# A mixed stage in a one-layer decoder step: the first query batch, the page table, the peer keys and two page groups move into the stage before it

## The chip, the cores and the metric

The kernel runs on one NeuronCore of a Trainium2 chip, in one launch. Its time is the device time of the whole execution in microseconds (us); lower is better. The engines are TensorE (PE; its weight loads are PEld), VectorE (DVE), ScalarE (ACT), GpSimd (POOL) and SyncE (SP); here SyncE only issues DMAs and waits for them, and its queue is SPq in the rows. Each engine works off its own instruction stream in order, and semaphores tie the streams together.

## The reference

One inference step of a one-layer decoder for a prompt of 1024 tokens and 8 samples of 8 new tokens, model width 1024. Only what the change touches stands here:

```
mix = concat([attention, rglru], -1) @ w_out
x1 = layer_norm(alpha * x + mix, ln1_g, ln1_b)
ffn = peer_ffn(x1, peer_wq, peer_keys, peer_u, peer_v)
...
def block(tb):                                   # 128 tokens
    q = (tb @ wq).reshape(128, 8, 2, 128)        # 8 retrieval heads, two halves
    sc = jnp.einsum('thpd,hpnd->thpn', q, keys)  # 128 keys for each half
    s1, i1 = lax.top_k(sc[:, :, 0], 16)
    s2, i2 = lax.top_k(sc[:, :, 1], 16)
    cand = s1[..., :, None] + s2[..., None, :]
    top_s, top_p = lax.top_k(cand, 16)           # 16 of 16384 experts
    g = softmax(top_s)
    act = gelu(einsum('td,thkd->thk', tb, u_tab[eidx]))
    return einsum('thk,thkd->td', g * act, v_tab[eidx])
...
past_k = cache_k[page_table]                     # samples: 32 pages of 128 keys each
```

The attention is differential (two softmax maps per head). Everything is float32.

## The kernel before

The kernel is a row of blocks. A block ends when all five engines have arrived at a barrier, and the next begins there.

**The mix block** (function `prompt_attention_mix`, up to 654 us) computes the prompt's attention, and then, for eight tiles of 128 tokens in the order `TILES` = 4 to 7, 0 to 3, the product with `w_out` on TensorE (`half_mix`, L877) and the layer norm on VectorE (last instruction L1077). This is x1. It lies in `res[g % 2]` and SyncE stores it to `x1_scratch` in DRAM (L783), waits until the store has landed, and loads the x row for the tile after next. The first four of these tiles, the *dense* ones, are also transposed into `x1Td` in SBUF. Three slices of the query weights `peer_wq` (one per retrieval head) are loaded into the ring `ring` here. The PSUM banks `S[0]` and `S[1]` (`a_s`) take the products of alternate tiles.

**The mixed stage** (first block of `peer`, 654 to 1461 us) is laid out in slots by a planner that runs when the program is built. All engines walk the slots in the same order. Each of the eight samples has 32 slots:

- *Sample attention.* In slots 0 to 15 of a sample TensorE transposes its 32 key pages (`page_turn_pe`, L1557), ScalarE copies them out (L1567), and every fourth page is followed by scores. Slot 16: scores of the new keys (L1589). Slots 17 to 19: softmax on VectorE (it makes `cj`, L1608, the scale of the weights) and the exponential on ScalarE. Slots 20 to 31: the weights' transposes (L1621) and the products with the value pages. The pages come in groups of four (`GP`) through a ring `pg` in `w_room`; SyncE reads each page's number from `pt`, the page table in SBUF, before it issues the load. `pt` is loaded at the block's start.
- *Queries.* 16 batches of 16 matmuls of 128x512 each (`q_pe`, L1320), placed by the table `Q_AT`: 8 in each of slots 0 and 1, none in slots 2 to 7, after that mostly one in a slot, three in slots 16 to 19 of a sample. A batch is one head for four tiles. Batches of *dense* tiles read `x1Td`; batches of *gathering* tiles (0 to 3) read `x1T[1]`, which is made in slots 9 and 10 (`X_TURN_AT`) by transposes (L1285) of x1 rows that SyncE loads back from `x1_scratch` (`load_xn`); VectorE (L1294) and ScalarE copy them out. ScalarE copies each half batch of queries (L1328), TensorE multiplies with the transposed keys (`score_pe`, L1369), ScalarE copies the scores (L1377).
- *Keys.* The 16 key matrices are loaded by two DMAs at the second page group and transposed in slots 2 and 3 (`KEY_TURN_AT`); ScalarE copies them (L1307).
- *Ranking*, on VectorE, 17 steps for each batch (`RANK_STEPS`): eight searches of 16 best (`top16`, L1382 to L1389), the pairs (L1402, L1405), four more searches, place, index twice, gate (L1482). Its slots come out of a planner with a cost for each step. The first batch is ranked in slots 5 to 15.
- *Scatters*, on GpSimd: when a dense batch is ranked, 48 indirect DMAs of 128 gates each (`scatter_pool`, L1782) add them into `gate_scratch` in DRAM, for three of the four dense tiles; eight heads make 384. The fourth dense tile's gates become one-hot matrices on VectorE and ScalarE in the last sample's slots and after (`QUAD_AT`), and matmuls on TensorE (L1839).
- *End.* After slot 255 the samples' outputs are folded by TensorE in slot 257 (L1857, behind VectorE's L2000), mixed, normalised, and one more small batch of queries and scores is made. SyncE then loads the first gates (L2031, L2036).

**The last stage** (1461 us to the end) runs 128 chunks of 128 experts for the dense tiles on TensorE (L2044 transposes, L2058 and L2090 products) and beside it the gathers of 16 experts per token and head for the other tiles on GpSimd, with VectorE.

A q step (one matmul of 128x512) has two records in the trace, a transpose has one.

## Time and profile before

| what | value |
|---|---|
| median of 3 runs | 3581.18 us |
| the runs | 3580.72, 3581.18, 3588.79 us |
| profiled execution, its own time | 3575.43 us |
| its span in the trace | 3573.7 us |
| TensorE busy over the span | 3357.5 us (94%) |
| VectorE busy | 2622.8 us (73%) |
| GpSimd busy | 2051.8 us (57%) |
| ScalarE busy | 842.2 us (24%) |
| DMA, mean over the span | 286 GB/s |
| mixed stage | 654.2 to 1461.3 us |
| last stage | 1461.3 to 3573.7 us |

The trace is of one execution, with times from the span's start. Busy shares are means over stages with different limits. A timeline row stands for one or more like instructions of an engine: when they start, how long they last in all, and in brackets the idle time of the engine just before them and what ended it. Granted clock means the share of TensorE's full clock that the chip gave in that stretch.

### The profile page before, as it was taken

To read this page: it belongs to the slowest core of one execution; us is meant where nothing else is said; L and a number is where in the kernel's file an instruction comes from. 1 tells how busy PE (TensorE), PEld (TensorE's weight loads), DVE (VectorE), ACT (ScalarE), POOL (GpSimd) and SP (SyncE) were. 2 spreads that over 40 slices of the span, in tenths; PEclk is the share of its full clock that TensorE was granted. 3 is DMA by queue.
4 is the path that set the end of the run, shared out by engine and by line. 5 is a ranking of instruction groups with operands and counts; after the bars stand their busy time and mean duration, and the time that the engine had idled before them with its cause. 6 is when DMAs were issued, how large, how long until landed. Compare 5 with 4: busy or idle time off the path is not lost.

```text
span 3573.7 us, 41306 instructions
## 1 busy us (share of the span) xinstructions
PE 3357.5 (94%) x12551; PEld 1744.3 (49%) x12551; DVE 2622.8 (73%) x5429; ACT 842.2 (24%) x1786; POOL 2051.8 (57%) x1620
## 2 busy tenths in 40 slices
PE   8999799799899977799999999999999999999898
PEld 5676464444444445444444444444444444444343
DVE  3444584467778766578887888888888888888884
ACT  2333560344443465111111111111111111111021
POOL 0000100078888888577777777777777677777540
PEclk9999899899999988899999999999999999999999
DMA  4000631588889885899999999999999999999961
GB/s 148 30 29 15 243 146 68 179 213 213 205 211 233 226 229 147 263 396 407 405 407 398 400 406 404 403 394 406 406 406 404 396 391 407 405 401 398 355 218 42
DMA packets 410615, 1023.34 MB, mean 286 GB/s; under 512 B 93965, under 2 KB 130030, under 8 KB 406834
## 3 DMA queue, kind: packets, MB, share of 16 engines
q0 software_dynamic: 221184, 604.27, 46.6%
q1 hardware_dynamic: 175138, 394.69, 31.5%
q10 hardware_dynamic: 14096, 22.02, 1.7%
q8 instruction: 90, 1.47, 0.2%
q14 instruction: 107, 0.88, 0.1%
HBM read 972.05 MB, written 48.77 MB: 286 GB/s over the span
## 4 chain that ended last, share of the span: by engine, by line
POOL 21%; DMA 19%; issue 9%; DVE 7%; PE 2%; ACT 0%; DVEq 0%; SPq 0%; ACTq 0%; POOLq 0%
DMA u<-in_peer_u,idx_all 19%; POOL v L2165 11%; POOL u L2157 10%; DVE u L2175 2%; DVE facc L2203 2%; PE e_b L2319 1%; PE e_b L2090 1%; DVE wq L2203 1%; DMA w_room<-x_scratch 1%; DVE k_room L2105 1%; PE e_b L2307 0%; DVE ln_st L1060 0%; DVE w_room L2389 0%; DVE w_room L1073 0%; DVE w_room L2360 0%
## 5 line engine op out<-in xcount | busy, mean ns | idle before, releaser
L2157 POOL DMA_INDIRECT u<-in_peer_u,idx_all x576 | 724.8, 1258 | 393.2 <-DVE act L2175 246.4
L2090 PE MATMUL e_b<-w_room,e_room 128*128 128x512 f32 x2048 | 908.1, 597 | 21.7 <-DVE k_room L2105 12.8
L2175 DVE CUSTOM_DVE_ANT_0 u<-u,xb 128x1024 f32<-128x1024 f32 x576 | 705.7, 1225 | 295.1 <-DMA u<-in_peer_u,idx_all 268.5
L2058 PE MATMUL e_b<-wq 128*128 128x512 f32 x2048 | 900.3, 592 | 0.0
L2165 POOL DMA_INDIRECT v<-in_peer_v,idx_all x576 | 690.5, 1199 | 214.1 <-issue 177.5
L1782 POOL DMA_INDIRECT gate_scratch<-e_room,slot_of x384 | 610.4, 1590 | 188.3 <-issue 120.9
L2090 PEld LDWEIGHTS e_b<-w_room,e_room 128*128 128x128 f32 x2048 | 390.9, 191 | 519.4 <-issue 491.8
L2058 PEld LDWEIGHTS e_b<-wq 128*128 128x128 f32 x2048 | 379.5, 190 | 429.0 <-issue 429.0
L2203 DVE SCALAR_TENSOR_TENSOR facc<-v,w,facc 128x1024 f32<-128x1024 f32 x317 | 406.5, 1282 | 1.4
L2203 DVE SCALAR_TENSOR_TENSOR wq<-v,w,wq 128x1024 f32<-128x1024 f32 x254 | 325.9, 1283 | 0.5
L2051 ACT ACTIVATE wq<-e_b 128x512 f32<-128x512 f32 x256 | 140.0, 594 | 722.3 <-PE e_b L2044 473.2
L2064 ACT ACTIVATE wq<-e_b 128x512 f32<-128x512 f32 x128 | 76.5, 597 | 745.3 <-PE e_b L2058 599.7
L812 POOL MEMSET qz<- 128x1024 f32 x1 | 1.0, 951 | 375.8 <-POOLq L110 375.8
L445 PE MATMUL p_bank<-w_in,wq 128*128 128x512 f32 (+1 forms) x432 | 186.9, 592 | 0.0
L2105 DVE TENSOR_TENSOR k_room<-k_room,e_b 128x512 f32<-128x512 f32 x248 | 158.4, 678 | 6.7 <-PE e_b L2090 6.7
L2044 PEld LDWEIGHTS e_b<-ident,wq 128*128 128x128 f32 x1024 | 121.0, 142 | 80.0 <-issue 79.9
L1567 ACT ACTIVATE w_room<-e_b 128x512 f32<-128x512 f32 x256 | 139.8, 597 | 55.0 <-PE e_b L1557 46.8
L2044 PE MATMUL e_b<-ident,wq 128*128 128x128 f32 x1024 | 134.4, 275 | 12.9 <-PEq L2398 12.9
L2319 PE MATMUL e_b<-wq,e_room 128*128 128x512 f32 (+1 forms) x288 | 133.7, 620 | 13.4 <-DVE w_room L2379 6.9
L1320 PE MATMUL e_b<-wq 128*128 128x512 f32 x256 | 128.2, 615 | 11.4 <-PEq L110 11.1
L1320 PE MATMUL e_b<-v,wq 128*128 128x512 f32 x256 | 132.5, 621 | 0.9 <-PE e_b L1648 0.7
L439 PE MATMUL p_bank<-wq,w_in 128*128 128x128 f32 (+1 forms) x1152 | 132.0, 277 | 0.9 <-issue 0.9
(387 smaller groups left out, 3543.4 us busy)
## 6 DMA issues: line engine op xcount, KB each, us to landing
wq<-in_peer_u SPq DMA_DIRECT2D x128, 512.0 KB
w_room<-in_peer_v SPq DMA_DIRECT2D x128, 512.0 KB, 22.6
w_room<-in_cache_v SPq DMA_DIRECT2D x144, 256.0 KB
w_room<-in_cache_k SPq DMA_DIRECT2D x128, 256.0 KB
gate_scratch<-zeros SPq DMA_DIRECT2D x24, 1024.0 KB, 27.0
wq<-gate_scratch SPq DMA_DIRECT2D x96, 256.0 KB
u<-in_cache_k SPq DMA_DIRECT2D x64, 256.0 KB
xb<-in_cache_k SPq DMA_DIRECT2D x64, 256.0 KB
```

The costliest lines, as they stand in the source:

```text
L445: last = pe.matmul(bank[0:R, :], xT[:, k, 0:R], w_in[:, k, col:col + AW], start=(k == 0), stop=(k == KC - 1))
L1320: last = pe.matmul(B[m][:], ring[h % NR][:, k, m * P:m * P + P], x1T[group][:, k, :], start=(k == 0), stop=(k == KC - 1))
L1782: pool.indirect_dma_start(gate_d[m].rearrange("e (t o) -> (e t) o", o=1), bass.IndirectOffsetOnAxis(ap=slot_of[:, m, h, j:j + 1], axis=0), ...
L2044: last = pe.transpose(TQ[r][:, k * P:k * P + P], Ud[c % NUD][:, at:at + P], ident[:])
L2058: last = pe.matmul(AQ[c % 2][:, 0:DT], UT[c % 2][:, k, :], x1Td[:, k, :], start=(k == 0), stop=(k == KC - 1))
L2090: last = pe.matmul(OQ[i % 2][b][:], WT[n % 2][:, c, m * P:m * P + P], Vd[(4 * n + c) % NVD][:, b * 512:b * 512 + 512], start=(c == 0), sto ...
L2105: dve.tensor_tensor(part, part, OQ[i % 2][b][:], ALU.add).then_inc(s["dadd"], 1)
L2157: pool.indirect_dma_start(u[x % NU], None, a["peer_u"], bass.IndirectOffsetOnAxis(ap=idx_all[:, t, h, j:j + 1], axis=0)).then_inc(s_u[x % ...
L2165: pool.indirect_dma_start(v[y % NV], None, a["peer_v"], bass.IndirectOffsetOnAxis(ap=idx_all[:, t, h, j:j + 1], axis=0)).then_inc(s_v[y % ...
L2175: dve.tensor_tensor_reduce(u[x % NU], u[x % NU], xb[t % 2][:], 1.0, 0.0, ALU.mult, ALU.add, act16[k % 2][:, j:j + 1]).then_inc(s["ufree"], 1)
L2203: dve.scalar_tensor_tensor(out=dst, in0=v[y % NV], scalar=w, in1=dst, op0=ALU.mult, op1=ALU.add).then_inc(s["vfree"], 1)
L2319: last = pe.matmul(Z[h][0:R, :], x2T[q % 2][:, k, 0:R], wg[:, k, h * 512:h * 512 + 512], start=(k == 0), stop=(k == KC - 1))
```

## The change

1. **First queries.** The 16 matmuls of batch 0 are issued at the end of TensorE's part of the mix block, after the last `half_mix`. They write to the banks of `S[0]`, which now live on as `q_banks` into the next block. In that block `Q_AT` begins with batch 1: two matmuls in each of slots 2 to 9, none in 10 to 15, then the old pattern. ScalarE copies batch 0's queries in slots 0 and 1, its scores are made in slots 1 and 2, and its ranking goes to slots 1 to 11 (was 5 to 15). By the planner's rules all other batches come earlier too: batch 13, the last dense one, is ranked by slot 214 (was 223), the last batch in slots 233 to 247 (was 244 to 267).
2. **Early loads.** SyncE loads the page table at the mix's start, the keys after the first x1 store (into `keys_in`), and the first two page groups, eight pages, after the second and the third (into `early`), all in free room of `wq`. The ring of page groups is counted from the third on.
3. **Stores of x1.** The last two are no longer waited for on SyncE in the mix; their landing is waited for by GpSimd at the start of the next block and by SyncE before it loads x1 rows.
4. **Keys and x1 transposes.** `KEY_TURN_AT` has all four key steps in slot 0, `X_TURN_AT` all four tiles in slot 15, and the loads of x1 rows for it come with page group 6 instead of groups 1 and 2.

```diff
             def load_early(sp, g):
+                if g == 0:
+                    kv = a["peer_keys"].rearrange("(g q p) d -> g p q d", q=8, p=P)
+                    for n in range(2):
+                        sp.dma_start(keys_in[:, n, :].rearrange("p (q d) -> p q d", q=8), kv[n]).then_inc(s_early, 16)
+                elif g <= NEARLY:
+                    if g == 1:
+                        sp.wait_ge(s_pt, 16)
+                    for n in range(GP):
+                        at = (g - 1) * GP + n
+                        page = sp.value_load(pt[0:1, at:at + 1], min_val=0, max_val=a["cache_k"].shape[0] // PAGE - 1)
+                        sp.dma_start(early[g - 1][:, n, :], a["cache_k"][bass.ds(page * PAGE, PAGE), :]
+                                     ).then_inc(s_early, 16)
...
                 for g in range(NT):
                     sp.wait_ge(sx["x1"], g + 1)
-                    sp.dma_start(rows(x1_d, TILES[g] * P, P), res[g % 2][:]).then_inc(s_st[g % 2], 16)
-                    sp.wait_ge(s_st[g % 2], 16 * (g // 2 + 1))
+                    done = s_st[g % 2] if g + 2 < NT else s_x1st
+                    sp.dma_start(rows(x1_d, TILES[g] * P, P), res[g % 2][:]).then_inc(done, 16)
+                    load_early(sp, g)
                     if g + 2 < NT:
+                        sp.wait_ge(done, 16 * (g // 2 + 1))
                         sp.wait_ge(sx["xt"], 2 * min(g + 1, NDT))
                         load(g + 2)
...
+                pe.wait_ge(sx["sum"], NT - 1)
+                pe.wait_ge(sx["xe"], 2 * NDT)
+                pe.wait_ge(s_wq[0], 16)
+                for m in range(2):
+                    for k in range(KC):
+                        pe.matmul(B[0][m], ring[0][:, k, m * P:m * P + P], x1Td[:, k, :],
+                                  start=(k == 0), stop=(k == KC - 1))
...
-        KEY_TURN_AT = {2: (0, 1), 3: (2, 3)}
-        X_TURN_AT = {9: (0, 1), 10: (2, 3)}
+        KEY_TURN_AT = {0: (0, 1, 2, 3)}
+        X_TURN_AT = {15: (0, 1, 2, 3)}
...
-            n = 8 if x < 2 else 0 if x < 8 else 3 if 16 <= c < 20 else 0 if c % 8 == 7 or c in (3, 11, 27) else 1
+            n = 0 if x < 2 else 2 if x < 10 else 0 if x < 16 else 3 if 16 <= c < 20 else 0 if c % 8 == 7 or c in (3, 11, 27) else 1
...
-            ready = Q_DONE[e, 1] + 4
+            ready = Q_DONE[e, 1] + 4 if e else 1
...
                 def rows_between(G):
-                    if G == 1:
-                        kv = a["peer_keys"].rearrange("(g q p) d -> g p q d", q=8, p=P)
-                        for g in range(2):
-                            sp.dma_start(v[6 + g].rearrange("p (q d) -> p q d", q=8), kv[g]).then_inc(s["kr"], 16)
-                        for n in range(2):
+                    if G == NEARLY + NPB:
+                        sp.wait_ge(s_x1st, 32)
+                        for n in range(UN):
                             load_xn(sp, n)
-                    if G == 2:
-                        for n in range(2, UN):
-                            load_xn(sp, n)
-
-                sp.dma_start(pt[:], a["page_table"]).then_inc(s["pt"], 16)
-                sp.wait_ge(s["pt"], 16)
+
+                sp.wait_ge(s_pt, 16)
...
             @block.gpsimd
             def _(pool):
+                pool.wait_ge(s_x1st, 32)
                 pool.memset(qst, 0.0)
```

TensorE, from the last product of the mix into the mixed stage, before (L1320 are queries, L1557 page transposes):

```order
L877 MATMUL a_s<-w_out,mixA 128x512 [waits s_p_r]
L877 MATMUL a_s<-w_out,mixA 128x512 x7
L779 UNCONDITIONAL_BRANCH
L2448 UNCONDITIONAL_BRANCH [waits barrier_Pool_Activation_PE_DVE_SP_release]
L1320 MATMUL e_b<-wq 128x512 [waits s_wq0]
L1320 MATMUL e_b<-wq 128x512 x7
L1557 MATMUL e_b<-ident,w_room 128x128 [waits s_p_hc]
L1557 MATMUL e_b<-ident,w_room 128x128 x3
L1557 MATMUL e_b<-ident,w_room 128x128 [waits s_p_hc]
L1557 MATMUL e_b<-ident,w_room 128x128 x3
L1320 MATMUL e_b<-wq 128x512 x8
```

and now (L947 are queries, L1336 key transposes, L1597 page transposes):

```order
L904 MATMUL a_s<-w_out,mixA 128x512 [waits s_p_r]
L904 MATMUL a_s<-w_out,mixA 128x512 x7
L947 MATMUL q_banks<-wq 128x512 [waits s_wq0,s_dve,s_pool]
L947 MATMUL q_banks<-wq 128x512 x15
L803 UNCONDITIONAL_BRANCH
L2484 UNCONDITIONAL_BRANCH [waits barrier_Pool_Activation_PE_DVE_SP_release]
L1336 MATMUL e_b<-ident,wq 128x128 [waits s_early]
L1336 MATMUL e_b<-ident,wq 128x128 x7
L1336 MATMUL e_b<-ident,wq 128x128 [waits s_e_kte]
L1336 MATMUL e_b<-ident,wq 128x128 x3
L1336 MATMUL e_b<-ident,wq 128x128 [waits s_e_kte]
L1336 MATMUL e_b<-ident,wq 128x128 x3
```

The sixteen query matmuls stand ahead of the block's end, and the new block opens with sixteen key transposes ahead of the first pages.

ScalarE, from the start of the mixed stage, before (L1548 and L1550 the sample's queries and keys, L1567 page copies, L1328 query copies, L1307 key copies):

```order
L2453 UNCONDITIONAL_BRANCH [waits barrier_Pool_Activation_PE_DVE_SP_release]
L1548 ACTIVATE w_room<-qTs 64x8 [waits s_e_zero,s_e_S]
L1548 ACTIVATE w_room<-qTs 64x8 x7
L1550 ACTIVATE w_room<-kTs 128x32
L1567 ACTIVATE w_room<-e_b 128x4x128 [waits s_e_ktp,s_e_S]
L1567 ACTIVATE w_room<-e_b 128x4x128 [waits s_e_ktp]
L1328 ACTIVATE k_room<-e_b 128x512 [waits s_e_q]
L1567 ACTIVATE w_room<-e_b 128x4x128 [waits s_e_ktp] x2
L1307 ACTIVATE k_room<-e_b 128x512 [waits s_e_kt] x2
L1328 ACTIVATE k_room<-e_b 128x512 [waits s_e_q]
```

and now (L1341 key copies, L1362 query copies, L1588 and L1590 the sample's queries and keys, L1607 page copies, L1411 score copies):

```order
L1341 ACTIVATE k_room<-e_b 128x512 [waits s_e_kt,s_e_zero]
L1341 ACTIVATE k_room<-e_b 128x512 [waits s_e_kt] x3
L1362 ACTIVATE k_room<-q_banks 128x512
L1588 ACTIVATE w_room<-qTs 64x8 [waits s_e_S]
L1588 ACTIVATE w_room<-qTs 64x8 x7
L1590 ACTIVATE w_room<-kTs 128x32
L1607 ACTIVATE w_room<-e_b 128x4x128 [waits s_e_ktp,s_e_S]
L1607 ACTIVATE w_room<-e_b 128x4x128 [waits s_e_ktp]
L1362 ACTIVATE k_room<-q_banks 128x512
L1607 ACTIVATE w_room<-e_b 128x4x128 [waits s_e_ktp] x2
L1411 ACTIVATE e_room<-e_b 128x512 [waits s_e_sc]
```

Keys and queries are copied first, the sample's queries behind them, and the first score copy comes right after the fourth page copy.

VectorE, in the middle of the first batch's ranking, before (L1382 to L1389 a search, L1294 copies of transposed x1, L1402 and L1405 the pairs):

```order
L1387 MAX tv<-wq 128x8 [waits s_e_ch]
L1389 MAX_INDEX ti<-tv,wq 128x8 [waits s_e_ch]
L1294 COPY v<-e_b 128x4x128 [waits s_e_xt] x2
L1402 CAST tif<-ti 128x128 [waits s_e_ch]
L1405 TENSOR_TENSOR wq<-tv 128x4x64
L1405 TENSOR_TENSOR wq<-tv 128x4x48
L1294 COPY v<-e_b 128x4x128 [waits s_e_xt,s_e_ch]
L1294 COPY v<-e_b 128x4x128 [waits s_e_xt]
L1382 MAX ts<-wq 128x8
```

and now (L1416 to L1423 a search, L1436 and L1439 the pairs):

```order
L1421 MAX tv<-wq 128x8 [waits s_e_ch]
L1423 MAX_INDEX ti<-tv,wq 128x8 [waits s_e_ch]
L1436 CAST tif<-ti 128x128 [waits s_e_ch]
L1439 TENSOR_TENSOR wq<-tv 128x4x64
L1439 TENSOR_TENSOR wq<-tv 128x4x48
L1416 MAX ts<-wq 128x8 [waits s_e_ch]
```

The copies of transposed x1 no longer stand between the searches.

## Rows read from the trace of the kernel before

**Rows 1.** Stretches of 100 us: length, busy PE, PEld, DVE, ACT, POOL, granted clock, DMA share, GB/s.

```profile
700.00:800.00 100.00, 93.31 (x549) 48.20 (x547) 70.13 (x282) 46.47 (x91) 66.79 (x43) 1.00 0.81 209
1700.00:1800.00 100.00, 100.00 (x276) 47.35 (x275) 83.82 (x117) 11.44 (x23) 72.85 (x59) 1.00 1.03 406
```

**Rows 2.** GpSimd's timeline (start, duration), first and last scatter; their group on the page.

```profile
720.19 1.74 POOL L1782 DMA_INDIRECT gate_scratch<-e_room,slot_of  x1 [65.42 <-DVE e_room L1482]
...
1451.91 1.54 POOL L1782 DMA_INDIRECT gate_scratch<-e_room,slot_of  x1 [0.30 <-issue]
...
L1782 POOL DMA_INDIRECT gate_scratch<-e_room,slot_of x384 | 610.4, 1590 | 188.3 <-issue 120.9
```

**Rows 3.** Timelines of TensorE and SyncE at the mixed stage's end; SyncE's waits.

```profile
1447.30 1.09 PE L1369 MATMUL e_b<-k_room 128*64 128x128 f32 x16 [0.79 <-ACT k_room L1377]
...
1461.30 3.81 PE L2044 MATMUL e_b<-ident,wq 128*128 128x128 f32 x16 [12.91 <-PEq L2398]
...
1449.43 0.45 SPq L2031 DMA_DIRECT2D wq<-gate_hot  x1
...
1455.49 3.74 SPq L2036 DMA_DIRECT2D wq<-gate_scratch  x3
...
SPq L2036 <- DMA gate_scratch<-e_room,slot_of: 8.3, 3, 5.6
```

**Rows 4.** TensorE's timeline from the mix's last product into the mixed stage.

```profile
636.14 7.03 PE L877 MATMUL a_s<-w_out,mixA 128*128 128x512 f32 x16
...
654.25 9.78 PE L1320 MATMUL e_b<-wq 128*128 128x512 f32 x16 [11.08 <-PEq L110]
...
664.74 7.03 PE L1320 MATMUL e_b<-wq 128*128 128x512 f32 x16
```

**Rows 5.** VectorE and SyncE there; SyncE's wait for stores (sum, count, longest).

```profile
648.89 1.22 DVE L1077 TENSOR_TENSOR res<-res,b 128x1024 f32<-128x1024 f32 x1
...
SPq L783 <- DMA x_scratch<-res: 4.4, 2, 2.2
...
665.90 3.66 SPq L1532 DMA_DIRECT2D w_room<-in_cache_k  x4
```

**Rows 6.** VectorE's timeline, the ranking of batch 0.

```profile
682.30 0.30 DVE L1382 MAX8 tv<-e_room 128x8 f32<-128x128 f32 x1 [26.90 <-ACT e_room L1377]
...
694.88 0.67 DVE L1294 COPY v<-e_b 128x512 f32<-128x512 f32 x1
...
697.49 0.69 DVE L1405 TENSOR_TENSOR wq<-tv 128x256 f32<-128x256 f32 x2
...
703.46 0.27 DVE L1382 MAX8 ts<-wq 128x8 f32<-128x112 f32 x1
...
719.67 0.23 DVE L1482 TENSOR_TENSOR e_room<-e_room,zx 128x64 f32<-128x64 f32 x1
```

**Rows 7.** ScalarE's first row of the stage; the page copies' group on the page.

```profile
654.92 1.74 ACT L1548 ACTIVATE w_room<-qTs 64x8 f32<-64x8 f32 x8 [8.37 <-POOL pcol L2443]
...
L1567 ACT ACTIVATE w_room<-e_b 128x512 f32<-128x512 f32 x256 | 139.8, 597 | 55.0 <-PE e_b L1557 46.8
```

**Rows 8.** A stretch of 10 us at the stage's start, columns as in rows 1.

```profile
650.00:660.00 10.00, 5.75 (x7) 2.45 (x8) 0.68 (x5) 1.88 (x9) 0.53 (x3) 0.52 0.28 98
```

**Rows 9.** TensorE's timeline at single places; its wait for the weights' scale.

```profile
695.60 1.11 PE L1285 MATMUL e_b<-ident,v 128*128 128x128 f32 x4 [3.63 <-DVE v L1294]
...
706.10 1.12 PE L1557 MATMUL e_b<-ident,w_room 128*128 128x128 f32 x8 [0.40 <-ACT w_room L1567]
...
721.34 0.25 PE L1589 MATMUL e_b<-w_room 128*32 128x8 f32 x8 [0.72 <-issue]
...
1295.27 0.25 PE L1589 MATMUL e_b<-w_room 128*32 128x8 f32 x8 [0.83 <-ACT wq L1584]
...
1356.47 3.33 PE L1857 MATMUL e_b<-w_room,sel 128*32 128x512 f32 x4 [7.95 <-DVEq L2000]
...
PE e_b L1621 <- DVE cj L1608: 10.2, 4, 4.0
```

More of the change, by code:

```diff
@@ L50 @@
 NR = 3
+GP = 4
+NEARLY = 2
 NSC = 3
@@ L138, in program @@
         room = wq[:].rearrange("p k n -> p (k n)")
+        early = [room[:, (10 + 2 * n) * D:(12 + 2 * n) * D].rearrange("p (g d) -> p g d", g=GP) for n in range(NEARLY)]
+        keys_in = room[:, 14 * D:16 * D].rearrange("p (n d) -> p n d", n=2)
         kT, qT, v_all, spare = [room[:, n * 4 * D:(n + 1) * 4 * D] for n in range(4)]
@@ L742, in prompt_attention_mix @@
         res = [sb(f"res{n}", [P, D]) for n in range(2)]
-        S = [ps(f"a_s{m}", (P, 2 * 512)) for m in range(2)]
+        S = [q_banks, ps("a_s1", (P, 2 * 512))]
         TB = [ps(f"a_t{n}") for n in range(2)]
@@ L1232, in peer @@
         ln2 = LayerNorm(sb, sem, "ln2", g2, b2)
-        B = [ps(f"e_b{n}") for n in range(8)]
+        B = [q_banks[:, 512 * n:512 * n + 512] for n in range(2)] + [ps(f"e_b{n}") for n in range(2, 8)]
         ACC, QB, TB, KB, SB_, OB = B[0:2], B[2], B[3], B[4:6], B[6], B[7]
@@ L1301, in keys_pe @@
                 m = 4 * t + c
-                last = pe.transpose(B[2 + t % 2][:, c * P:c * P + P], v[6 + m // 8][:, (m % 8) * P:(m % 8) * P + P], ident[:])
+                last = pe.transpose(B[2 + t % 2][:, c * P:c * P + P], keys_in[:, m // 8, (m % 8) * P:(m % 8) * P + P], ident[:])
             last.then_inc(s["kt"], 1)
@@ L1325, in q_act @@
         def q_act(act, e, m):
-            act.wait_ge(s["q"], 2 * e + m + 1)
+            wait(act, s["q"], 2 * (e - 1) + m + 1)
             wait(act, s["sc"], 2 * (e - 2) + 2)
@@ L1355, in score_pe @@
                 pe.wait_ge(s["kte"], 4)
-            if e == 1 and r == 0:
+            if e == 2 and r == 0:
                 pe.wait_ge(s["xTa"], UN)
@@ L1519, in pages @@
                 at = turn_of(i, G)
-                dst, done = (late_pages, s_late) if G == LATE_G else (pg[at % NPB], s_pg[at % NPB])
+                if at < NEARLY:
+                    continue
+                room = (at - NEARLY) % NPB
+                dst, done = (late_pages, s_late) if G == LATE_G else (pg[room], s_pg[room])
                 src = a["cache_k"] if G < NG else a["cache_v"]
@@ L1527, in pages @@
                 for n in range(GP):
-                    if G != LATE_G and at >= NPB:
+                    if G != LATE_G and at >= NPB + NEARLY:
                         page_free(sp, at - NPB, n)
@@ L1538, in page_group @@
             at = turn_of(i, G)
+            if at < NEARLY:
+                return early[at]
+            at -= NEARLY
             pe.wait_ge(s_pg[at % NPB], 16 * GP * (at // NPB + 1))
@@ L1696, in peer @@
         Q_AT, Q_DONE = {}, {}
-        x, step = Q_FIRST, 0
+        Q_DONE[0, 0] = Q_DONE[0, 1] = 0
+        x, step = Q_FIRST, 2 * KC
         while step < NBAT * 2 * KC:
             c = x % SEQ_SLOTS
-            n = 8 if x < 2 else 0 if x < 8 else 3 if 16 <= c < 20 else 0 if c % 8 == 7 or c in (3, 11, 27) else 1
+            n = 0 if x < 2 else 2 if x < 10 else 0 if x < 16 else 3 if 16 <= c < 20 else 0 if c % 8 == 7 or c in (3, 11, 27) else 1
             for _ in range(min(n, NBAT * 2 * KC - step)):
@@ L1720, in peer @@
         for e in range(NBAT):
-            ready = Q_DONE[e, 1] + 4
+            ready = Q_DONE[e, 1] + 4 if e else 1
             for name, n in RANK_STEPS:
-                first_slot = ready + (2 if name == "top" and n >= 4 else 0)
+                first_slot = ready + ((2 if e else 1) if name == "top" and n >= 4 else 0)
                 if slot < first_slot:
```

30 lines of the change are left out of this document (19 added, 11 removed), and 2 rows, old and new, of the table names.

## The prediction

> **What bounds the kernel now.** I read the stretches of the whole span first. In the last of the kernel's stages TensorE is busy 100.00 of 100 us [rows 1]; there the order of work is the same before and after, so what starts it earlier should end it earlier. In the stage ahead of it, in which the sample attention, the queries and the ranking are mixed (I call it the mixed stage; it runs from 654.2 to 1461.3 us), no engine is full: TensorE 93, VectorE 70, GpSimd 67 of 100 us [rows 1]. So I went to the two ends of that stage, and asked which chain ends last.
>
> The timeline of GpSimd [rows 2] shows one unbroken chain. It sits idle 65.42 us until the first batch's last ranking step, scatters for the first time at 720.19, and for the last time at 1451.91 to 1453.45. Between them lie 384 scatters of 1590 ns, with an idle time of 120.9 us that is put down to issue; all of the 188.3 us idle before this line is 65.4 + 120.9 + 2, so after its start this engine never waited for a ranking to speak of. The chain is 733 us long and starts when batch 0 is ranked. SyncE's three loads of the gates wait 8.3 us in all for the last scatters to land, 5.6 us at the longest, and the next stage begins at 1461.30 [rows 3].
>
> TensorE's chain in the same stage ends with the scores at 1447.30 + 1.09, and a ScalarE copy of 0.6 follows [rows 3]. Had the scatters landed by then, SyncE would have issued its first gate load at 1449.43 as it did, and the three others in 1.3 us more (0.45 each); with the 2.1 us from the last load's issue to the stage's start seen now (1461.30 less 1455.49 + 3.74), the stage could have begun at 1453.2. So **TensorE's chain has a slack of 8.1 us, and the scatters have none.** A gain is the lesser of what the scatters' chain gains and 8.1 us plus what TensorE's chain gains.
>
> **When the stage starts.** The mix's last matmul ends at 643.17, VectorE's last normalisation at 650.11; the store of x1 is waited for some 2.2 us, and the stage begins at 654.21 [rows 4, 5]. Now 32 records of queries (16 matmuls, two records each) follow at 643.17. Sixteen such records take 7.03 us back to back (6.87 from start to start), so they end at 656.9. Their inputs are long there: the bank is free once tile 6 is summed, which is at the tile before. After them comes the passage to the next block, 1.5 us in the mix (652.7 to 654.2) or 2.1 us at the other end; I take 1.8, and the stage starts at 658.7, **4.5 us later**. The last x1 store, whose landing is now waited for by GpSimd alone, has 6 us by then and costs nothing. The eight page loads, two key loads and the page table go out between stores of the mix, whose loads for the tile after next have a tile of 13.7 us to land in; SyncE takes 3.66 us for four pages [rows 5], which lies beside it. Cost nothing; if that cover were gone it would be 7.3 us.
>
> **The scatters' chain.** Until now the ranking of batch 0 began at 682.30, 28.1 us into the stage, and its last step ended at 719.90 [rows 6]. Its own work is less than those 37.6 us: eight searches 12.58 us, the pairs 0.8, and from 703.46 on 16.4 with no gap, 29.8 in sum; the rest, near 8 us, went to x1 turns that stand between (VectorE waits there for TensorE, and TensorE for VectorE). These come at slot 15 now, behind this batch. The ranking's start is now bound by ScalarE: from the stage's start 0.7 us until its first instruction is released, four key copies of 0.6, a query copy 0.6, the sample's queries 1.74 and its keys 0.2, four page copies of near 0.6 (597 ns) [rows 7], another query copy 0.6, then a score matmul 1.0 and its copy 0.6: 9.4 us. Scatters start at 658.7 + 9.4 + 29.8 + 0.5 = 698.4, **21.8 us earlier**. The 384 scatters stay as they are. They won't start to wait: a head is 48 scatters, 92 us, so the last head's are due near 1340; by the planner the last dense batch is ranked at slot 214, and 32 slots take 82 us (new keys at 721.34 and, seven sequences on, 1295.27 [rows 9]), which puts it near 1220.
>
> **TensorE's chain**, term by term. (a) The stage starts later: -4.5. (b) The first batch's matmuls are gone from it: they took 9.78 (clock 0.52 after a pause) and 7.03 [rows 4, 8]: +16.8. (c) By slot 16, 32 query matmuls are to be done instead of 22, the first 16 of them outside: ten more than in the old slots 2 to 15, 10 x 0.86 = -8.6. Six of them fall where a slot without queries leaves a gap of 0.40 us [rows 9], +2.4. (d) The x1 turns cost a wait of 3.63 for VectorE [rows 9] and two short ones, near 4.5 in all; VectorE should be free at slot 15: +4.5. (e) At the start TensorE must now wait for ScalarE (query copies and sample queries, 0.6 + 2.0 + 1.1), which used to lie under the queries: -3.5. (f) With such gaps the clock falls; ten us with TensorE busy 5.75, after a pause, have a granted clock of 0.52 [rows 8], near the lower of its two levels (1.2 of 2.4 GHz). Sixteen records at the lower level cost 9.78 - 7.03: -2.8.
>
> The Trainium skill, page "TensorE: Matmul & The Clock Gate", section "HAM oscillation — how this bites in real kernels", says that work short enough to leave the array waiting after it lets the clock fall again, so that the next batch of matmuls starts at half rate. That speaks against moving the long matmuls away from this stage's start, and the fall after a pause in [rows 8] agrees. By it the term (f) stands; without it the sum is 2.8 us better.
>
> (g) At the end, slots 229 to 240 have ten query matmuls fewer, each leaving a gap of 0.40: 10 x 0.46 = +4.6. (h) The fold at slot 257 waits 7.95 us for VectorE [rows 9], which is then ranking batch 15 (two searches and the place, 4.9 us); that ranking now ends at slot 247: +4.9. (i) It stands instead around the last sequence's softmax and the first one-hot quads: in slots 243 to 246 VectorE has 9.2 us of place and index beside four quads of 1.2, against some 11.2 us of TensorE's work: a wait of 2.8, and a backlog of up to 3 at slot 240. Between 0 and -6, I take -4. Sum: -4.5 + 16.8 - 8.6 + 2.4 + 4.5 - 3.5 - 2.8 + 4.6 + 4.9 - 4 = **+9.8 us**, and with the slack 17.9.
>
> So both chains gain, and what is late next is TensorE's: the stage should end **18 us** earlier, 4 us ahead of what the scatters would allow. The profiled execution took 3575.43 us (span 3573.7 and 1.7 around it) and would take 3557.4; the median of the runs is 5.8 us above it (3581.18), so the forecast is 3563.2. About 0.3% (10.7 us) is what a measurement can tell from no change.
>
> **The unknown cost** is how the other batches' ranking falls against the eight softmaxes. All fifteen come some ten slots earlier. Now TensorE waits 10.2 us in 4 of them for the weights' scale, 4.0 at the longest [rows 9]. Bounds: nobody waits, +10; each of eight waits 4.0, 32 - 10.2 = -21.8. I take 0: the planner now puts about half as much ranking as before into slots 8 to 15, ahead of the softmax, and the two steps that now stand in slot 18 of most sequences lie under ScalarE's exponential.
>
> **Rivals.**
> 1. The forecast: TensorE's chain ends the stage, gain 11 to 21 (3560 to 3570). For it: both ends of the stage are in the rows. Chance 0.54.
> 2. The scatters alone bound the stage, because (f), (i) or the softmax waits turn out for the better: gain 21 to 25, centre 3558. Against it: TensorE's terms would all have to be good. Chance 0.14.
> 3. The ranking's new places take half of their bound, 11 us, at the softmaxes: gain 7, so 3574, within 0.3%. For it: 93 of 100 us busy means that each wait of VectorE or ScalarE is paid in full. A late first load in the last stage (its weights are asked for only some 8 us before it) would end here too. Chance 0.24.
> 4. Slower: the same mechanism at its bound and at ScalarE too. Each ranking makes ScalarE wait once for its place step, and page copies queue behind it; if in all eight sequences the scale is 4.0 late (-21.8) and sixteen such waits reach TensorE with 1.5 us more than now (-24), TensorE's chain ends 28 us later than forecast by (g) to (i), so 3581 - 18 + 46 = 3609. It decides from 17.9 us of new waits on; slower by over 0.3% needs 28.6. Against it: TensorE idles some 7 us in 100 now [rows 1], whatever the ranking's places, and its load is the same. Chance 0.08.
>
> **The numbers.** Faster by over 0.3%: 1 and 2, 0.68. Within: 0.24. Slower: 0.08. The range leaves out rival 4 and the outer tenth: 3553 (gain 25 and 3 us for the spread of runs) to 3578 (gain 7 with 4 us for the spread). The likeliest case's own is 3560 to 3570.
>
> **What would show it.** In the profile of the changed kernel: 32 records of queries at the mix's end and the mixed stage's first row near 658.7; the first scatter near 698 and the last near 1431; TensorE's last score near 1438.6, and no wait of SyncE for scatters; the stage's end near 1443. A granted clock near 0.5 in the stage's first ten us shows (f); a fold wait near 3 us shows (h). The sum is wrong if the first scatter comes after 705, if waits for the softmax's scale add up to more than 20 us, or if the last stage is longer than the 2112 us from 1461.3 to the end.

## The result, and the profile after

The changed kernel takes 3588.83 us (median of 12 runs, 3585.03 to 3595.32) where the kernel before took 3580.68 in the same sessions: a ratio of 1.0023 with a 95% interval of 1.0015 to 1.0031. It is **8 us slower, not 18 us faster**, and lies outside the range that was given.

The profiled execution has a span of 3583.2 us (before 3573.7). Its seam and the end of the mixed stage, in timelines of TensorE and GpSimd (start, duration, in brackets the idle time before the row and what ended it):

```profile
644.20 13.90 PE L947 MATMUL q_banks<-wq 128*128 128x512 f32 x32
659.39 1.06 PE L1336 MATMUL e_b<-ident,wq 128*128 128x128 f32 x8 [1.29 <-PEq L112]
...
698.62 1.74 POOL L1823 DMA_INDIRECT gate_scratch<-e_room,slot_of  x1 [38.71 <-DVE e_room L1516]
...
1418.35 1.55 POOL L1823 DMA_INDIRECT gate_scratch<-e_room,slot_of  x1 [0.30 <-issue]
...
719.00 0.25 PE L1629 MATMUL e_b<-w_room 128*32 128x8 f32 x8 [0.72 <-ACT wq L1624]
...
1311.65 0.25 PE L1629 MATMUL e_b<-w_room 128*32 128x8 f32 x8 [2.52 <-ACT wq L1624]
...
1462.54 1.09 PE L1403 MATMUL e_b<-k_room 128*64 128x128 f32 x16 [0.79 <-ACT k_room L1411]
1469.12 3.81 PE L2085 MATMUL e_b<-ident,wq 128*128 128x128 f32 x16 [5.49 <-PEq L2439]
```

They answer to [rows 2, 3, 4 and 9]. The seam did what was forecast: the stage begins at 659.4 (forecast 658.7) and the first scatter comes at 698.62 (forecast 698.4). The scatters end at 1419.9, 33.6 us earlier than before. But TensorE's last score ends at 1463.63 and not at 1438.6, and the next stage begins at 1469.12, 7.8 us later than before. From there to the end it takes 2114.1 us (before 2112.4). So the time was lost in the mixed stage, on TensorE. The scores of the new keys (slot 16 of each sequence) are milestones. In the first sequence they come 2.3 us earlier than before (719.00 against 721.34), in the last one 16.4 us later (1311.65 against 1295.27). **18.7 us were lost in the middle of the stage**, though there is less to do there: 221 query matmuls lie between the two milestones now (442 records), 231 before (462). In a second profile of the kernel before, which comes below, the middle is 6.8 us longer, and against that one the loss is 12.0 us.

What TensorE and ScalarE waited for in the mixed stage (sum, count, longest):

```profile
PE e_b L1597 <- ACT w_room L1607: 39.0, 29, 7.0
PE e_b L1617 <- ACT w_room L1607: 14.7, 7, 7.1
PE e_b L1661 <- DVE cj L1648: 9.7, 6, 6.3
...
ACT e_room L1492 <- DVE e_room L1456: 45.9, 12, 7.8
```

The same three waits in the kernel before, whose lines have other numbers:

```profile
PE e_b L1557 <- ACT w_room L1567: 10.7, 16, 3.1
...
PE e_b L1577 <- ACT w_room L1567: 6.6, 3, 4.4
...
ACT e_room L1458 <- DVE e_room L1422: 23.8, 8, 4.4
```

TensorE's wait for the weights' scale (9.7, before 10.2 in [rows 9]) has not moved. Its wait for ScalarE's page copies has gone from 17.3 to 53.7 us, and ScalarE's own wait, for VectorE's place step ahead of the exponential, from 23.8 to 45.9. One such place, in the timelines of VectorE, ScalarE and TensorE:

```profile
923.20 0.23 DVE L1516 TENSOR_TENSOR e_room<-e_room,zx 128x64 f32<-128x64 f32 x1
923.35 0.29 DVE L1416 MAX8 tv<-e_room 128x8 f32<-128x128 f32 x1
...
944.96 0.23 DVE L1456 TENSOR_TENSOR e_room<-ts 128x64 f32<-128x64 f32 x1
...
936.45 1.08 ACT L1607 ACTIVATE w_room<-e_b 128x512 f32<-128x512 f32 x2 [0.59 <-PE e_b L1597]
945.22 0.26 ACT L1492 ACTIVATE e_room<-e_room 128x64 f32<-128x64 f32 x1 [7.68 <-DVE e_room L1456]
...
938.64 1.09 PE L1597 MATMUL e_b<-ident,u 128*128 128x128 f32 x8
946.59 1.94 PE L1597 MATMUL e_b<-ident,u 128*128 128x128 f32 x8 [6.86 <-ACT w_room L1607]
948.32 1.92 PE L1354 MATMUL q_banks<-wq 128*128 128x512 f32 x2
```

VectorE goes from the last step of batch 5 (923.20) to the first search of batch 6 (923.35) with no pause; by the planner that search belongs to slot 29, and TensorE is in slot 0 of the next sequence by then. The place step comes at 944.96. ScalarE has done its page copies by 937.5 and stands 7.68 us at the exponential, which is next in its stream, with page copies behind it that have nothing to do with ranking. Both PSUM banks for pages are then full, and TensorE stands 6.86 us. The rows behind the pause take 1.94 and 1.92 us where such rows take 1.04 and 1.02 (granted clock 0.50 in the stretch from 946.6 to 950.0).

TensorE stands like this once in each of seven sequences, 2.90, 6.98, 6.86, 7.14, 6.30, 3.84 and 2.37 us, 36.4 in all. They belong to the even batches, 2 to 14. The planner's slots point at the reason. Before, the rankings of batches 0 to 10 start in slots 5, 23, 41, 54, 72, 86, 102, 118, 133, 149 and 164, 13 to 18 apart. Now they start in 1, 13, 28, 50, 61, 82, 93, 110, 122, 141 and 153, from batch 3 on by turns 11 or 12 and 17 to 22 apart. The second of a close pair is due some 11 slots of 2.4 us (26 us) behind the first, whose own work is 29.8 us. In the trace of the changed kernel batches 4, 6, 8, 10, 12 and 14 start right behind the batch before them, with no idle time of VectorE. The kernel before has two such pairs near its end (batch 12 is 13 slots behind batch 11, batch 14 is 12 behind batch 13), and there stand its two longest waits of TensorE for page copies, 3.14 and 4.37 us.

Distance is not all that the table changes. Batch 2 stands 15 slots behind batch 1 and waits too: batch 1's ranking has the sample's softmax inside it and lasts 42.8 us (702.93 to 745.72). And in the kernel before batch 3 is 13 slots behind batch 2 and VectorE is not late for it: these slots take in a sample's slots 16 to 19 with three queries each, and the two rankings start 40.7 us apart (780.82 and 821.50). So it is the distance in time that counts, against all that VectorE has to do in it.

### The profile page after: what moved, and what is told of

It is laid out like the page before. It is cut to its first block, busy times and chain, and to the rows that moved or that the text cites. A ratio compares the mean times of both kernels' runs of the same rounds, so it can differ in the third digit from the quotient of the medians.

```text
span 3583.2 us, 41297 instructions
## 1 busy us (share of the span) xinstructions
PE 3362.4 (94%) x12551; PEld 1747.1 (49%) x12551; DVE 2622.5 (73%) x5429; ACT 840.8 (23%) x1785; POOL 2049.7 (57%) x1620
## 4 chain that ended last, share of the span: by engine, by line
PE 20%; DMA 15%; POOL 13%; issue 6%; DVE 5%; ACT 0%; DVEq 0%; SPq 0%; ACTq 0%
DMA u<-in_peer_u,idx_all 15%; PE e_b L2099 8%; POOL v L2206 6%; POOL u L2198 6%; PE q_banks L2131 5%; PE e_b L2131 4%; PE e_b L2360 1%; PE e_b L2085 1%; DVE facc L2244 1%; DVE u L2216 1%; DMA w_room<-x_scratch 1%; DVE k_room L2146 0%; PE e_b L2348 0%; DVE w_room L2430 0%; DVE ln_st L1094 0%
## 5 line engine op out<-in xcount | busy, mean ns | idle before, releaser
L2099 PE MATMUL e_b<-wq 128*128 128x512 f32 x2048 | 900.6, 593 | 0.0
L2131 PE MATMUL q_banks<-w_room,e_room 128*128 128x512 f32 x1024 | 459.6, 602 | 18.9 <-DVE k_room L2146 9.7
L2131 PE MATMUL e_b<-w_room,e_room 128*128 128x512 f32 x1024 | 451.7, 594 | 3.6 <-DVE k_room L2146 3.6
L2131 PEld LDWEIGHTS q_banks<-w_room,e_room 128*128 128x128 f32 x1024 | 197.0, 193 | 272.2 <-issue 250.8
L2131 PEld LDWEIGHTS e_b<-w_room,e_room 128*128 128x128 f32 x1024 | 194.9, 191 | 249.9 <-issue 243.3
L1607 ACT ACTIVATE w_room<-e_b 128x512 f32<-128x512 f32 x256 | 139.8, 597 | 41.8 <-PE e_b L1597 40.1
L462 PEld LDWEIGHTS p_bank<-wq,w_in 128*128 128x128 f32 x1152 | 131.9, 195 | 1.3 <-issue 1.3
## 6 DMA issues: line engine op xcount, KB each, us to landing
wq<-gate_scratch SPq DMA_DIRECT2D x96, 256.0 KB, 16.6
```

The source lines that it names most:

```text
L462: last = pe.matmul(bank[:, c * P:c * P + R], w_in[:, k, col + c * P:col + c * P + P], xT[:, k, 0:R], start=(k == 0), stop=(k == KC - 1))
L1607: act.activation(kTp[:, :, n * P:n * P + P], KB[c % 2][:].rearrange("p (h t) -> p h t", h=H), ACT.Copy).then_inc(s["ktpe"], 1)
L2099: last = pe.matmul(AQ[c % 2][:, 0:DT], UT[c % 2][:, k, :], x1Td[:, k, :], start=(k == 0), stop=(k == KC - 1))
L2131: last = pe.matmul(OQ[i % 2][b][:], WT[n % 2][:, c, m * P:m * P + P], Vd[(4 * n + c) % NVD][:, b * 512:b * 512 + 512], start=(c == 0), sto ...
```

## The experiments

Theory A: the loss is ScalarE's wait in order for the place step. Its cause (A2) is that the query table now brings the rankings in close pairs. (The table moves each ranking against the sample's softmax and page copies too. No run changes the distances alone, so the runs test the table as a whole.) Rivals: B, VectorE's lateness costs the same by another way (softmax); C, the loss lies at the seam, in the early loads or in the last stage. All times are medians; the kernel before had 3581.25, 3579.83 and 3575.99 in the three sessions, so runs of different sessions are compared by their ratios to it.

**Exponentials later.** The wait is left as it is, and the exponential goes to the slot of the gate step:

```diff
-                if (name, n) == ("index", 0):
+                if name == "gate":
                     EXP_AT.setdefault(slot, []).append(e)
```

> The changed kernel, with each dense or gathering batch's exponential on ScalarE issued in the slot of the batch's gate step instead of the slot of its first index step (two or three slots later); nothing else moves. In the changed kernel's trace ScalarE waits 4.57, 7.80, 7.68, 7.50, 7.12, 4.39 and 3.75 us for VectorE's place step of the even batches, and TensorE then waits 2.90, 6.98, 6.86, 7.14, 6.30, 3.84 and 2.37 us (36.4 in all) for page copies that stand behind that wait on ScalarE. Theory A (these in-order waits of ScalarE are where the forecast gain went): they go, TensorE's last score comes some 30 us earlier (near 1433), the next stage begins near 1438, and the time is 30 us below the changed kernel's, near 3558, which is under the kernel before. Theory B (VectorE itself is late, so TensorE only waits somewhere else, at the softmax's scale or the new keys): the waits for the scale grow by as much, and the time stays within 8 us of 3589. Theory C (the loss lies at the seam or in the last stage): no change, 3589.

Measured: 3556.68, ratio 0.9932 (0.9913 to 0.9952), 32 us below the changed kernel. Waits of the mixed stage, and the end of it:

```profile
PE e_b L1597 <- ACT w_room L1607: 15.9, 21, 3.2
PE e_b L1661 <- DVE cj L1648: 9.0, 6, 5.4
...
ACT e_room L1492 <- DVE e_room L1456: 4.6, 2, 3.1
...
1422.32 1.09 PE L1403 MATMUL e_b<-k_room 128*64 128x128 f32 x16 [0.79 <-ACT k_room L1411]
1443.56 2.74 PE L2085 MATMUL e_b<-ident,wq 128*128 128x128 f32 x11 [20.15 <-PEq L2439]
...
1438.10 1.54 POOL L1823 DMA_INDIRECT gate_scratch<-e_room,slot_of  x1 [0.30 <-issue]
```

ScalarE's wait is nearly gone, the scale's wait has not grown, and TensorE's chain ends 40 us earlier. That is 4 us more than the seven waits; behind each of them eight like records took 1.93 to 1.94 us in the changed kernel. A holds, B and C fall. The stage begins 5 us later than expected, since the scatters end last now.

**Half of it.** The exponential in the slot of the second index step, one or two slots later than in the change.

> The changed kernel with the exponential in the slot of the second index step, one slot later for batches 4, 6 and 12, two for batches 2, 8, 10 and 14 (the late exponentials were one more again). A slot is some 2.4 us there. ScalarE's waits of 4.57, 7.80, 7.68, 7.50, 7.12, 4.39 and 3.75 should shrink by that to about 0, 5.4, 5.3, 2.7, 2.3, 2.0 and 0, TensorE's 36.4 us to about 14, and the time falls to near 3567, between 3589 and 3557. If only the last slot counts, it stays near 3589.

Measured: 3562.29, ratio 0.9953 (0.9938 to 0.9969).

```profile
ACT e_room L1492 <- DVE e_room L1456: 15.1, 4, 5.0
```

4.96, 4.46, 3.10, 2.61 and 2.78 us remain for batches 4, 6, 8, 10 and 12 (expected 5.4, 5.3, 2.7, 2.3 and 2.0; the trace puts the last one down to issue). One slot took 2.8 and 3.2 us off the wait of batches 4 and 6, two slots 4.4 and 4.5 us off that of batches 8 and 10, and one slot 1.6 us off that of batch 12: about a slot's time for a slot. The time follows, 25 us below the change (expected 22).

**The kernel before with late exponentials.**

> The kernel before with the same edit alone: the exponential in the slot of the gate step. Theory A with the slack as the prediction had it (scatters have none, TensorE's chain has 8.1 us): TensorE's waits for page copies get smaller (17.3 us in the mixed stage before), its last score comes up to 12 us earlier, but the last scatter stays at 1452 and the next stage at 1461, so the time is within 2 us of the kernel before. Theory D (TensorE's chain bounds the stage before, the scatters don't): the time falls by what TensorE's chain gains, 5 to 12 us.

Measured: 3575.77, ratio 0.9986 (0.9975 to 0.9997). Its waits for page copies shrank, but in the profiled execution the last score ended at 1448.3 all the same. What was won by slot 240 (7.6 us) went again in the stretch behind it, where the granted clock was 0.81 (0.86 in the first profile of the kernel before). The next stage came 12.3 us behind the last score, as in that first profile, so in this execution the scatters bound; the time fell by 5 us all the same. Neither theory as it stands fits both. The run shows that the same edit which gives 32 us in the changed kernel gives at most 9 in the one before.

**The old places.** The queries of batches 1 to 15, and with them the rankings, go back to the slots that they had; the rest of the change stays. (The x1 transposes then need to wait for batch 0's scores only.)

```diff
-            n = 0 if x < 2 else 2 if x < 10 else 0 if x < 16 else 3 if 16 <= c < 20 else ...
+            n = 0 if x < 8 else 3 if 16 <= c < 20 else ...
```

> The changed kernel with the query table and so the ranking's slots of batches 1 to 15 as in the kernel before (no query steps in slots 0 to 7, batch 1 from slot 8 on); batch 0's queries stay at the end of the mix, its ranking stays in slots 1 to 11, early loads, key and x1 transposes stay. Theory A: no wait of 5 us or more for page copies; TensorE's last score near 1438, next stage near 1444, the time near 3564, some 25 us below the changed kernel. Theory C (the seam is to blame): the time stays near 3589.

Measured: 3563.29, ratio 0.9957 (0.9942 to 0.9973), 24 us below the change.

```profile
PE e_b L1597 <- ACT w_room L1607: 10.7, 13, 2.6
...
ACT e_room L1492 <- DVE e_room L1456: 25.7, 10, 4.7
...
1448.41 1.94 PE L2085 MATMUL e_b<-ident,wq 128*128 128x128 f32 x8 [6.01 <-PEq L2439]
```

The long waits are gone (4.57 us is the longest) though the exponentials stand where the change has them relative to their batch. In the profile TensorE's chain is 10.8 us ahead of the changed kernel's by slot 16 of the first sequence (708.16 against 719.00), with ten query matmuls fewer up to there, and gains 11.4 us more in the middle, although those ten stand there. So the table is what costs: seam, early loads and the new places of keys and x1 together gain 15 us, and the table takes them back and more.

**The table alone,** in the kernel before:

```diff
-            n = 8 if x < 2 else 0 if x < 8 else 3 if 16 <= c < 20 else ...
+            n = 8 if x < 2 else 0 if x < 8 else 2 if x < 16 else 3 if 16 <= c < 20 else ...
```

> The kernel before with one part of the change alone: the query table brought forward by ten steps (two in each of slots 8 to 15), so that from batch 3 on every query and ranking has the slot it has in the changed kernel; the seam, the early loads, the key and x1 transposes stay as before. Theory A2 (rankings in pairs 11 to 13 slots apart, VectorE behind, ScalarE waiting in order for the place step in slots 0 to 5 of each sequence): six waits of TensorE for page copies of 3 to 7 us appear as in the changed kernel (18.7 us in the middle of the stage there), with ten more query steps (8.6 us) ahead; the stage ends 15 to 20 us later, the time is near 3597. Theory C (the early part of the change is to blame, not the table): within 5 us of the kernel before.

Measured: 3607.47, ratio 1.0080 (1.0064 to 1.0097).

```profile
ACT e_room L1458 <- DVE e_room L1422: 42.4, 9, 9.7
...
1484.38 1.94 PE L2044 MATMUL e_b<-ident,wq 128*128 128x128 f32 x8 [5.47 <-PEq L2398]
```

TensorE stands 8.85, 7.36, 6.61, 2.28, 6.30, 4.09 and 2.45 us ahead of page transposes, in the same places. (The trace puts the second, the third and the last down to issue; ScalarE stands for the place step beside them, 8.18, 7.43 and 3.82 us.) The stage's end is 23 us later than in the first profile of the kernel before and 19 later than in the second. By the ratios the time rose by 29 us where 16 were expected. Direction and place are those of A2; the size was taken too small.

**Both remedies together.**

> The changed kernel with both: the queries and rankings of batches 1 to 15 in the places of the kernel before, and the late exponentials. Theory A2 (the loss is one thing: rankings bunched 11 to 13 slots apart leave VectorE behind, and ScalarE's in-order wait passes that on to TensorE; either edit cuts it): the two gains, 25 and 32 us, don't add. The time is 3555 to 3563. If they were two separate losses it would be near 3540, as far as the scatters let it (their chain would end near 1436, so no less than 3552).

Measured: 3559.82, ratio 0.9942 (0.9924 to 0.9961). The gains of 24 and 32 us don't add: it is one loss. The scatters don't hide a second one, for the last score ends at 1434.98, behind the last scatter (1428.94). With late exponentials alone the time was 3 us lower, within the two intervals.

**The seam.** Batch 0's queries go back into slot 0 of the mixed stage, all else is the change.

> The changed kernel with one part undone: batch 0's sixteen query matmuls stand in slot 0 of the mixed stage again (behind the key transposes), not at the end of the mix; all slots stay. The mixed stage should begin near 654, and the first score comes some 12 us later than in the changed kernel. Theory A and the sums of the prediction: the matmuls cost TensorE's chain 14 to 17 us in the stage, less the 5 us of the earlier start, so 8 to 12 us more than the changed kernel, near 3598; the scatters end some 12 us later, near 1432, and still don't bound. Theory C (the matmuls at the mix's end are the loss): the time falls to 3580 or below.

Measured: 3597.96, ratio 1.0053 (1.0033 to 1.0073), 11 us above the changed kernel. The first scatter came at 706.63 (8 us later) and the stage began at 654.38. So the queries at the mix's end are worth 11 us, near the forecast's own terms (16.8 less 4.5).

**The x1 transposes** back to slots 9 and 10:

> The changed kernel with the x1 transposes back in slots 9 and 10 (and the x1 rows loaded with the third page group). The prediction gave the move to slot 15 some 8 us of the scatters' chain and 4.5 us of TensorE's. Then the first scatter comes 6 to 8 us later (near 706) and TensorE's chain ends 3 to 5 us later: the time is near 3593. If VectorE's lateness hides it, no change (3589).

Measured: 3592.51, ratio 1.0037 (1.0023 to 1.0052), some 5 us above the change, and the first scatter came at 705.02 instead of 698.62: 6.4 us, where the prediction said 8 (7.4 when the 1.0 us is added by which this execution is ahead at the stage's start, 664.45 against 665.43). The time is near the one expected, but not by the way expected. The scatters end at 1430.28, long before the last score (1474.51), and TensorE reaches slot 16 of the first sequence 3.0 us earlier than in the changed kernel (715.98 against 719.00), 2.0 us earlier without that lead. In slot 15 the transposes wait too, five times and 2.8 us in all. The time is lost behind that. In this profile the rows that start from 729.20 to 740.36 run at the lower clock (1.80 to 2.05 us where such rows take 1.04 to 1.10), with no pause over 0.8 us in the 30 us ahead of them. So where the 5 us come from stays open.

**Which chain bounds the end.** One scatter column less in each head (24 scatters, 46 us), with late exponentials and in the kernel before:

```diff
-            for j in range(TOPK):
+            for j in range(TOPK - 1):
                 for m in range(NSC):
```

> The changed kernel with the late exponentials and one scatter column less (the sixteenth gate of the three dense tiles left out). With late exponentials alone TensorE's last score ended at 1423.4 and the last scatter at 1439.6, and the next stage began at 1443.56. If the scatters bound it there, TensorE's chain takes over: the next stage begins near 1429, 14 us earlier, and the time is near 3543. If they don't, it stays at 3557.

> The kernel before with one scatter column less: each head scatters 15 of its 16 gates (360 scatters instead of 384), so the sixteenth gate of the three dense tiles is left out of the gate matrices; nothing else changes. 24 scatters of 1.91 us are 46 us. If the scatters alone bound the mixed stage's end and TensorE's chain has 8.1 us of slack, the next stage begins 8 us earlier (near 1453) and the time falls by 8 us. If TensorE's chain bounds the stage (no slack), nothing changes; if scatters were all that bounds it, the time would fall by 46.

> The kernel before itself, one more profiled execution. In the first profile TensorE's last score ended at 1448.4 and the last scatter at 1453.45; with 24 scatters less TensorE's last score came at 1459.5 and the next stage at 1465.1. If executions of one kernel differ by some 10 us in TensorE's chain, this one shows the last score anywhere between 1448 and 1460; if the first profile is typical, within 2 us of 1448.4.

With late exponentials: 3546.30, ratio 0.9905 (0.9887 to 0.9924), 10 us less, and the stage began at 1428.62, 15 us earlier. There the scatters did bound it. In the kernel before: 3578.22, ratio 0.9995 (0.9984 to 1.0006), where 8 us less were expected if the slack was real, and none if it wasn't. The profiles say why. TensorE's last score and the next stage in the second profile of the kernel before, its last scatter, and TensorE's rows of the one with fewer scatters:

```profile
1459.21 1.98 PE L1369 MATMUL e_b<-k_room 128*64 128x128 f32 x16 [0.78 <-ACT k_room L1377]
1465.29 2.95 PE L2044 MATMUL e_b<-ident,wq 128*128 128x128 f32 x12 [4.09 <-PEq L2398]
...
1455.14 1.54 POOL L1782 DMA_INDIRECT gate_scratch<-e_room,slot_of  x1 [0.30 <-issue]
...
1458.43 1.09 PE L1369 MATMUL e_b<-k_room 128*64 128x128 f32 x16 [0.79 <-ACT k_room L1377]
1465.14 3.17 PE L2044 MATMUL e_b<-ident,wq 128*128 128x128 f32 x13 [5.61 <-PEq L2398]
```

In these two executions TensorE's chain ends at 1461.2 and 1459.5, against 1448.4 in the first profile [rows 3], and it is TensorE, 4 to 6 us ahead of the stage, that bounds it. **The slack of 8.1 us was that of one execution.** By the ratio above, leaving out 24 scatters is worth at most 6 us, so the kernel before has no such slack as a rule. The 5 us of its late exponentials fit this: their stage began at 1460.60, 4.7 us before that of the second profile.

**The version that beats both.** Late exponentials for batches 1 to 15, batch 0's as in the change, so that the first scatter isn't delayed:

```diff
-                if (name, n) == ("index", 0):
+                if (name, n) == (("gate", 0) if e else ("index", 0)):
```

> The changed kernel with the late exponentials for batches 1 to 15, and batch 0's exponential where the change has it (slot of its first index step). In the first slots VectorE is not late, and the late exponential put the first scatter from 698.62 to 702.33. If the scatters bound the stage's end with late exponentials, their chain starts 3.7 us earlier and the time falls by as much, to 3553; if TensorE's chain bounds it, nothing changes (3557).

Measured: 3549.23, ratio 0.9911 (0.9896 to 0.9927), 7 us below the late exponentials alone (expected 4; the two intervals overlap), 40 below the change. The last scatter ends at 1426.65 and the last score at 1424.64, near together; but the stage begins only at 1434.68, 10.0 us behind the last score where it follows by 5.5 when TensorE bounds it, and SyncE waits 5.1 us for scatters. So the scatters still end last, by some 4 us. They began 4.9 us earlier than with the late exponentials alone and ended 13.0 us earlier; 6.0 of the 8.1 us between are waits of GpSimd for scatters of its own to land (11.2 us there, 5.2 here, none in the changed kernel). What makes these longer or shorter stays open.

## Why the prediction was wrong

Point by point, against its own steps:

- **The stage's start and the scatters' start**: right (658.7 and 659.4; 698.4 and 698.62). The scatters' pace was taken as unchanged, and they ended at 1419.9 instead of 1431: 721 us for 384, before 733. This does not come from the seam: with the table alone in the kernel before they took 721 too, with the old places in the changed kernel 733, and with the new table and late exponentials 737. So they took least in the profiles in which TensorE and ScalarE stand most; by what way, no run tells.
- **TensorE, terms (a) to (f)**: forecast +4.3 us by slot 16 of the first sequence, measured +2.3. The clock did not fall at the start as (f) had it: from 660 to 690 us it was granted in full, and the pause ahead was only 1.29 us long. (With the queries back in the stage the pause was 8.74 us, and the first eight transposes took 1.94.) The pause for ScalarE (2.64 us at 665.43, term (e)) came as said, though the parts of (e) add up to 3.7 and not to 3.5. Term (d) had the x1 transposes in slot 15 gain 4.5 us; they wait there as well, and going by one profile each, in the changed kernel slot 16 comes some 2 us earlier with the transposes in slots 9 and 10. So that the sum came near is luck in part: (d) was too good and (f) too bad.
- **Terms (g) to (i)**: (h) and (i) lie behind the new keys of the last sequence: forecast +0.9, measured +1.1 (153.1 us from there to the last score before, 152.0 now). The fold's wait fell from 7.95 to 3.04 as (h) said. The slots of (g), 229 to 240, lie ahead of that milestone, so its +4.6 were due in the middle of the stage.
- **The unknown cost**: here it failed. It was taken as 0 for the new places of the rankings. The middle of the stage should have become 4.6 us shorter by (g) and became 18.7 us longer, so the cost was 23.3 us (16.6 against the second profile of the kernel before). Its lower bound, -21.8, is near this by luck, for it counted another mechanism: waits for the softmax's scale, whose sum did not change. What came was ScalarE standing in order for a late place step, and TensorE for page copies behind it: 53.7 us of such waits, before 17.3. The step said that all fifteen rankings come some ten slots earlier, and looked at where they fall against the softmax. It did not look at how far apart they fall. The spacing was to be had from the planner before any run: 11 slots for work of 29.8 us.
- **Rival 4** named the wait that decides, ScalarE's in-order wait for the place step with page copies behind it. Its price was spread evenly (sixteen waits of 1.5 us more), and it had a chance of 0.08. It came as seven of 2.4 to 7.1 us, and the time of 3588.83 is 8 us slower than before, where this rival had 28.
- **The slack**: taken as 8.1 us. In the two first profiles it held (the next stage now follows TensorE's last score by 5.5 us, before by 12.9), so there the sum is -15.2 + 7.4 = -7.8. Against a second execution of the kernel before it is not there. What the change would have gained with an unknown cost of 0 no run gives: with the old table it gained 15 us, and with late exponentials but for batch 0's, which also take waits away that the kernel before had, 32.
- **What would show it wrong**: the prediction looked for waits at the scale above 20 us, a late first scatter, or a longer last stage. None of the three came; it had set no mark for page copies.

## What to carry to other kernels

When a table moves work that comes in lumps, compute the distance between the lumps in time, not only their new places: rankings 11 slots apart overran, where 14 to 18 slots in the kernel before had cost 2 us at most. Look also at what else lies within a lump, and at what waits behind its result: a ranking with a softmax inside made the next one late even at 15 slots. An instruction that waits for another engine should stand in its stream where its input is sure to be there, as long as its own result is wanted later: moving the exponentials by two or three slots was worth 32 us here. Its one cost was batch 0's, where VectorE was not late: the first scatter came 3.7 us later. And a slack read from one profiled execution should be checked in a second one before a sum is built on it.

## What was not expected of the hardware

Executions of one and the same kernel differ by where TensorE's clock falls. In both profiles of the kernel before TensorE waits some 2 us for the softmax's scale in one sequence, and goes on with the same 102 records. The wait and the first row behind it, of the first and the second profile, and each stretch with its length, TensorE's busy time and granted clock; last another such wait of the second profile:

```profile
981.02 0.22 PE L1621 MATMUL e_b<-cj,wq 128*8 128x32 f32 x2 [2.03 <-DVE cj L1608]
981.17 1.07 PE L1626 MATMUL e_b<-cj,wq 128*128 128x32 f32 x8
981.00:997.60 16.60, 16.58 (x102) 1.00 0.64 136
...
982.25 0.22 PE L1621 MATMUL e_b<-cj,wq 128*8 128x32 f32 x2 [2.22 <-DVE cj L1608]
982.40 1.91 PE L1626 MATMUL e_b<-cj,wq 128*128 128x32 f32 x8
982.20:1005.30 23.10, 23.05 (x102) 0.70 0.56 115
...
812.63 0.22 PE L1621 MATMUL e_b<-cj,wq 128*8 128x32 f32 x2 [2.26 <-DVE cj L1608]
812.78 1.08 PE L1626 MATMUL e_b<-cj,wq 128*128 128x32 f32 x8
```

After 2.03 us of idling the clock stayed; after 2.22 us it was at the lower level for part of 23 us, and the same work took 6.5 us longer. (In the kernel before with 24 scatters less, a wait of 2.12 us at this place was followed by 22.82 us for these records.) The length of the wait alone doesn't decide: the 2.26 us at 812.63, in the second profile too, left the clock in full. So a wait of two microseconds can cost two or nearly nine. The Trainium skill, page "TensorE: Matmul & The Clock Gate", section "HAM oscillation — how this bites in real kernels", says that pauses between bursts let the clock fall for what follows; the traces agree, and add that near such a pause the outcome changes from one execution to the next. The ends of TensorE's chain in the two profiles of the kernel before are 12.8 us apart (1448.4 and 1461.2); 6.5 of them lie in this stretch, and 4.6 behind the last sequence's new keys, where the granted clock was 0.86 in the one and 0.81 in the other.
